# The residual's turned blocks through device memory, issued from ScalarE's queue in place of SP's

## The chip, the cores and the metric

The kernel runs on one core of a Trainium2 chip. The metric is the device time of one execution in microseconds (us). The core has five engines that run their own instruction streams and meet at semaphores: TensorE (PE in the profile, its weight loads PEld), VectorE (DVE), ScalarE (ACT), GpSimd (POOL) and SyncE (SP), which here only issues DMA transfers. A name with a q behind it (SPq, ACTq) is an engine's issuing side.

## The reference

One sequence of 256 tokens of width 1024 in float32 passes through two blocks of two layers each. All of it adds to a residual `h`.

```python
# block 1: layer 0 with gated linear attention, layer 1 with differential attention
h = h + mix(rms_norm(h, norm_mix[i]))
h = h + swiglu(rms_norm(h, norm_ffn[i]), ffn_w_in[i], ffn_w_out[i])
gate = jax.nn.sigmoid(rms_norm(h, ple_norm[i]) @ ple_w_gate[i])
h = h + gate * (p[i] @ ple_w_proj[i])
# block 2: a short convolution, then a causal attention with ALiBi and a gate
h = h + short_conv_mixer(rms_norm_2(h, norm_g[0]), conv_w_in, conv_w, conv_w_out)
h = h + moba_mixer(rms_norm_2(h, norm_g[1]), attn_w_in, q_norm_g, k_norm_g, attn_w_out)
```

Each product of a normed `h` needs `h` with the model dimension on the partitions: `h` turned. The norm's row factor is applied to the product's result, its column gain to the turned `h`.

## The kernel before

**Weights.** All weights come as one stream of 297 units of 128 x 1024 float32 (512 KB), in the order in which they are used (`TILES` and `END`, lines 48 to 69: `END[t]` is the first unit of tile t). A unit passes through a ring of four in `raw`. SP fetches it (`fetch`, line 434) once VectorE is done with the unit four before it (semaphore `w_lo`). ScalarE rounds it to `whi`, VectorE takes the rest `wlo = raw - whi`, both in rings of eight (`split_to`, lines 665 and 1075). `split_to(n)` converts all units up to n that are not yet converted, so its argument sets how far an engine runs ahead of TensorE.

**Products.** TensorE multiplies every unit in three passes, `whi` by the upper part of the turned input, `wlo` by the upper part, `whi` by the lower part (`product`, line 1753): 12 matmuls of 128 x 512. The turned inputs are the pairs `X` and `Y`, each an upper part `[0]` and a lower part `[1]` with eight slices of 128 rows (kt 0 to 7), one for each 128 columns of `h`. A unit covers two slices. It waits for the upper part of its two slices before its first matmul (`upper`, line 1780) and for the lower part before its ninth (line 1799).

**How `h` is turned.** Some slices are turned on TensorE (`h_T`, line 1870) and copied out of PSUM by `lhs_hi` and `lhs_lo`. The others take a trip through device memory. VectorE transposes 32 x 32 squares of `h` into `h_blk` (`sblk` and `gblk` are two names for it), in two halves of 256 KB. Each half is written to DRAM and read back into `h_land` in another order, which completes the transpose. ScalarE then makes the upper part with the gain in it, VectorE the lower part. There are six such trips of two halves:

- three `second_blocks` trips into a mixer or attention input: into the first feed-forward (after the first mixer), into the second one, and into the last attention's input. The half q holds slices 4 + 2q and 5 + 2q. The halves are written by `second_blk` (line 1112) and read by `second_hi` (line 697) and `second_lo` (line 1123);
- one more `second_blocks` trip into the convolution's input (`CV_IN`);
- two `gate_blocks` trips, in the middle of the gated projection of either layer. The half t holds the tokens of 128 t and the slices 0 to 3. VectorE writes it at line 1404, ScalarE reads it at line 876 and VectorE at line 1414.

First products are ordered by `PAIR_ORDER`, so that the slices of a `second_blocks` trip are wanted from the fifth unit on, half 0 for the fifth and half 1 for the sixth.

**Who issues.** SP issues all transfers of these trips, between its fetches and in program order. It stops at each of them until the block is turned (`g_blk`) and, for the way back, until the half has landed in DRAM (`g_out0`, `g_out1`). Semaphores `g_land0` and `g_land1` tell ScalarE that a half is back. `g_hi` and `g_lhs` count upper and lower parts for TensorE.

```python
for q in range(2):
    sp.wait_ge(sem("g_blk"), 2 * r + q + 1)
    sp.dma_start(s_dram[s, q], sblk[:, q, :]).then_inc(sem(f"g_out{q}"), 16)
for q in range(2):
    sp.wait_ge(sem(f"g_out{q}"), 16 * (r + 1))
    sp.dma_start(sland[:, q, :, :], s_dram[s, q]...).then_inc(sem(f"g_land{q}"), 16)
```

**The squares.** Around each trip ScalarE also squares the half of `h` that was just completed, with a sum by row for the norm (`squares` and `square`, lines 708 to 720). They write `junk` and `stats`. GpSimd makes the row factor `rstd` of them.

GpSimd issues trips of its own in the last attention: 192 KB blocks of scores, `mb_blocks` out and `mb_pT` back (lines 624 to 636).

Of the kernel before, what the change touches and what calls it, by code (L numbers as in the profile page):

```python
# [23 lines left out]
P = 128  # L24
# [51 lines left out]
LAST = ((0, 0, NW), (1, 0, NW // 2), (1, NW // 2, NW))  # L76
PAIR_ORDER = ((0, 0), (0, 1), (1, 0), (1, 1), (0, 2), (0, 3), (1, 2), (1, 3))

# [162 lines left out]
def build(nc, stream, x, p, cols_d, rows_d, consts_d, wgate_d, out):  # L241
    ctx = ExitStack()
    with ctx:
# [147 lines left out]
        gblk = hblk[:, :].rearrange("p (t n) -> p t n", t=TT)  # L391
        gland = hland[:, :, :].rearrange("p i n -> p (i n)").rearrange("p (t i n) -> p t i n", t=TT, i=P // B)

# [6 lines left out]
        s_dram = nc.dram_tensor("second_blocks", (len(PAIRED), 2, P, NW), F32, kind="Internal").ap()  # L400
        g_dram = nc.dram_tensor("gate_blocks", (2, TT, P, NW), F32, kind="Internal").ap()
# [10 lines left out]
        def _(sp):  # L412
# [79 lines left out]
            def second_blocks(r, tile):  # L492

                at = END[tile] + (7 if tile == CV_IN else 8)
                fetch(done, at)
                s = PAIRED.index(tile)
                for q in range(2):
                    sp.wait_ge(sem("g_blk"), 2 * r + q + 1)
                    sp.dma_start(s_dram[s, q], sblk[:, q, :]).then_inc(sem(f"g_out{q}"), 16)
                for q in range(2):  # L500
                    sp.wait_ge(sem(f"g_out{q}"), 16 * (r + 1))
                    sp.dma_start(sland[:, q, :, :], s_dram[s, q].rearrange("q n -> (q n)")
                                 .rearrange("(i p w) -> p i w", i=P // B, p=P)).then_inc(sem(f"g_land{q}"), 16)
                return at

            def gate_blocks(n, tile):

                at = END[tile + 2] + 8
                fetch(done, at)
                for t in range(TT):  # L510
                    sp.wait_ge(sem("g_blk"), 2 * (2 * n + 1) + t + 1)
                    sp.dma_start(g_dram[n, t], gblk[:, t, :]).then_inc(sem(f"g_out{t}"), 16)
                for t in range(TT):
                    sp.wait_ge(sem(f"g_out{t}"), 16 * (2 * n + 2))
                    sp.dma_start(gland[:, t, :, :], g_dram[n, t].rearrange("q n -> (q n)")
                                 .rearrange("(i p w) -> p i w", i=P // B, p=P)).then_inc(sem(f"g_land{t}"), 16)
                return max(done, at)

# [7 lines left out]
            for n, (out_tile, tin) in enumerate(((GLA_OUT, FFN_IN0), (DF_OUT, FFN_IN1))):  # L526
                upto(done, END[out_tile])
                done = END[out_tile]
                done = second_blocks(2 * n, tin)
# [4 lines left out]
                done = gate_blocks(n, tin + FT + 2)  # L534
            done = second_blocks(4, CV_IN)
# [15 lines left out]
            done = second_blocks(5, MB_IN)  # L551
# [108 lines left out]
        def _(act):  # L660
# [26 lines left out]

            def mixer_lhs(j, dst, out):

                split_to(END[out + 4] - 1 + AHEAD + 1)  # L690
                lhs_hi(dst, norm_gain(j), (4, 5))
                squares(j, 0)
                split_to(END[out + 4] + 1 + AHEAD)
                squares(j, 1)
                second_hi(j, dst, 2 * (j - 1) // 3, END[out + 4])

            def second_hi(j, dst, r, base):

                split_to(base + 8)
                for q in range(2):  # L700
                    act.wait_ge(sem(f"g_land{q}"), 16 * (r + 1))
                    for k in range(2):
                        kt = 4 + 2 * q + k
                        A(dst[0][:, kt, :].rearrange("p (t i b) -> p t i b", t=TT, b=B),
# [108 lines left out]
            def ffn(n, src):  # L813
# [70 lines left out]
                if n == 1:  # L884
                    second_hi(j + 1, X, 4, END[CV_IN] - 1)
# [1497 lines left out]
```

## Time and profile before

| what | us |
|---|---|
| median of 3 runs | 901.86 |
| the runs | 900.85, 903.6, 901.86 |
| the profiled execution, whole | 900.89 |
| its span, first to last instruction | 898.7 |
| TensorE busy | 892.9 |
| VectorE busy | 654.6 |
| ScalarE busy | 506.1 |
| GpSimd busy | 63.4 |

The whole time of the profiled execution is 2.2 us longer than its span. Busy time counts an engine's instructions, not its waits and not the issuing of DMA transfers. TensorE's matmuls overlap in the record, so the mean of one (about 390 ns) is longer than the distance between two. In the views below a row that says x4 has merged four instructions in a row on the engine, and the first time is the first one's start. In square brackets stands the time that the engine was idle just before, and what ended it.

### The profile page before, as it was taken

To read this page: it belongs to the slowest core of one execution; us is meant where nothing else is said; L and a number is where in the kernel's file an instruction comes from. 1 tells how busy PE (TensorE), PEld (TensorE's weight loads), DVE (VectorE), ACT (ScalarE), POOL (GpSimd) and SP (SyncE) were. 2 spreads that over 40 slices of the span, in tenths; PEclk is the share of its full clock that TensorE was granted. 3 is DMA by queue.
4 is the path that set the end of the run, shared out by engine and by line. 5 is a ranking of instruction groups with operands and counts; after the bars stand their busy time and mean duration, and the time that the engine had idled before them with its cause. 6 is when DMAs were issued, how large, how long until landed. Compare 5 with 4: busy or idle time off the path is not lost.

```text
span 898.7 us, 12238 instructions
## 1 busy us (share of the span) xinstructions
PE 892.9 (99%) x4364; PEld 737.0 (82%) x4364; DVE 654.6 (73%) x997; ACT 506.1 (56%) x820; POOL 63.4 (7%) x75
## 2 busy tenths in 40 slices
PE   9999999999999999999999999999999999999998
PEld 8988888888888888778888888888888888887777
DVE  6985478777735699997787776646679897779764
ACT  6756555444444667688564444435664544587681
POOL 0001000000000003211100000000010000215100
PEclk9999999999999999999999999999999999999999
DMA  7674458766755655424487667746568775656621
GB/s 271 197 240 143 162 189 301 277 242 243 240 194 194 227 199 201 160 97 141 139 284 265 237 239 246 254 142 231 202 220 278 260 253 192 207 200 234 227 70 47
DMA packets 76988, 187.47 MB, mean 209 GB/s; under 512 B 6852, under 2 KB 31812, under 8 KB 76936
## 3 DMA queue, kind: packets, MB, share of 16 engines
q1 hardware_dynamic: 75480, 182.99, 59.6%
q0 software_dynamic: 1024, 3.15, 1.0%
q10 hardware_dynamic: 432, 0.66, 0.2%
q8 instruction: 31, 0.51, 0.2%
q14 instruction: 21, 0.17, 0.1%
HBM read 171.83 MB, written 14.94 MB: 208 GB/s over the span
## 4 chain that ended last, share of the span: by engine, by line
PE 95%; DMA 2%; issue 2%; DVE 1%; POOL 1%; ACT 0%; DVEq 0%; POOLq 0%
PE bank L1801 84%; PE bank L1839 3%; PE bank L1854 1%; PE bank L2114 1%; PE bank L2140 1%; DMA mb_pT<-mb_blocks 1%; DMA mb_blocks<-p_tok 1%; DMA h<-x_dram 0%; PE bank L2224 0%; PE bank L2125 0%; PE bank L2253 0%; PE bank L1961 0%; PE bank L2009 0%; PE bank L2013 0%; PE bank L2100 0%
## 5 line engine op out<-in xcount | busy, mean ns | idle before, releaser
L671 ACT ACTIVATE whi<-raw 128x1024 fp32r<-128x1024 f32 x295 | 306.2, 1060 | 186.3 <-DMA raw<-stream_dram 108.8
L1079 DVE TENSOR_TENSOR wlo<-raw,whi 128x1024 fp32r<-128x1024 f32 x295 | 347.5, 1213 | 55.6 <-ACT whi L671 54.8
L1801 PE MATMUL bank<-whi,x_hi 128*128 128x512 f32 x560 | 152.5, 394 | 0.0
L1801 PE MATMUL bank<-wlo,x_hi 128*128 128x512 f32 x560 | 149.9, 389 | 0.0
L1801 PE MATMUL bank<-whi,x_lo 128*128 128x512 f32 x560 | 149.8, 389 | 0.0
L1801 PEld LDWEIGHTS bank<-wlo,x_hi 128*128 128x128 f32 x560 | 105.1, 188 | 22.3
L1801 PEld LDWEIGHTS bank<-whi,x_lo 128*128 128x128 f32 x560 | 105.1, 188 | 22.0
L1801 PEld LDWEIGHTS bank<-whi,x_hi 128*128 128x128 f32 x560 | 103.4, 188 | 21.7 <-issue 1.2
L1801 PE MATMUL bank<-whi,y_hi 128*128 128x512 f32 x396 | 108.0, 394 | 0.1
L1801 PE MATMUL bank<-wlo,y_hi 128*128 128x512 f32 x396 | 106.0, 390 | 0.0
L1801 PE MATMUL bank<-whi,y_lo 128*128 128x512 f32 x396 | 106.0, 389 | 0.0
L1801 PEld LDWEIGHTS bank<-wlo,y_hi 128*128 128x128 f32 x396 | 74.3, 188 | 15.7
L1801 PEld LDWEIGHTS bank<-whi,y_lo 128*128 128x128 f32 x396 | 74.3, 188 | 15.7
L1801 PEld LDWEIGHTS bank<-whi,y_hi 128*128 128x128 f32 x396 | 72.8, 188 | 16.0 <-issue 0.8
L824 ACT ACTIVATE ffn_silu<-bank,rstd 128x256 f32<-128x256 f32 x44 | 18.4, 471 | 76.8 <-PE bank L1801 76.8
L1303 DVE SCALAR_TENSOR_TENSOR ffn_mid<-bank,rstd,ffn_silu 128x256 f32<-128x256 f32 x44 | 19.3, 479 | 54.0 <-ACT ffn_silu L824 54.0
L1801 PE MATMUL bank<-whi,mid_hi 128*128 128x512 f32 x176 | 47.0, 389 | 0.0
L1801 PE MATMUL bank<-wlo,mid_hi 128*128 128x512 f32 x176 | 47.0, 389 | 0.0
L1801 PE MATMUL bank<-whi,mid_lo 128*128 128x512 f32 x176 | 47.0, 389 | 0.0
L1109 DVE TENSOR_TENSOR h<-h,bank 128x512 f32<-128x512 f32 x22 | 14.1, 683 | 44.7 <-PE bank L1801 44.5
L579 POOL TENSOR_TENSOR ms<-stats 128x2 f32<-128x2 f32 x8 | 4.9, 611 | 577.1 <-ACT junk L718 577.1
L1801 PEld LDWEIGHTS bank<-wlo,mid_hi 128*128 128x128 f32 x176 | 33.0, 188 | 6.9
(251 smaller groups left out, 891.4 us busy)
## 6 DMA issues: line engine op xcount, KB each, us to landing
raw<-stream_dram SPq DMA_DIRECT2D x295, 512.0 KB, 4.6
ffn_blocks<-ffn_blk SPq DMA_DIRECT2D x22, 256.0 KB, 2.0
ffn_land<-ffn_blocks SPq DMA_DIRECT2D x22, 256.0 KB, 3.7
second_blocks<-h_blk SPq DMA_DIRECT2D x8, 256.0 KB, 2.0
h_land<-second_blocks SPq DMA_DIRECT2D x8, 256.0 KB, 3.1
cv_blocks<-cv_blk SPq DMA_DIRECT2D x7, 256.0 KB, 5.2
cv_land<-cv_blocks SPq DMA_DIRECT2D x7, 256.0 KB, 3.3
h_blocks<-h_blk SPq DMA_DIRECT2D x3, 512.0 KB, 6.3
```

What stands on the lines that cost most here:

```text
L579: step(nc.gpsimd.tensor_tensor(ms[:, j, 0, :], stats[:, j, 0, :], stats[:, j, 1, :], ALU.add))
L671: A(whi[:, u % RING, :], raw[:, u % RAW, :], ACT.Copy).then_inc(sem("w_hi"), 1)
L824: A(sg[:, (t - tin) % 2, k, :], bank[2 * (t % 2) + k][:, 0:256], ACT.Silu, scale=rstd[:, j, k:k + 1]).then_inc(sem("ffn_silu"), 1)
L1079: V.tensor_tensor(wlo[:, u % RING, :], raw[:, u % RAW, :], whi[:, u % RING, :].bitcast(F32), ALU.subtract).then_inc(sem("w_lo"), 1)
L1109: V.tensor_tensor(h[:, t, half * HALF:(half + 1) * HALF], h[:, t, half * HALF:(half + 1) * HALF], bank[2 * (tile % 2) + t][:, :], ALU.add) ...
L1303: V.scalar_tensor_tensor(mid[:, (t - tin) % 2, :, k, :], bank[2 * (t % 2) + k][:, 256:512].rearrange("p (k n) -> p k n", k=2), rstd[:, j, ...
L1801: last = T.matmul(bank[pair + t][:, :], lhs[a][:, kt, t * P:(t + 1) * P], w[:, u % RING, kk * NW:(kk + 1) * NW], start=part != 1 and k == ...
L1839: last = T.matmul(bank[pair + hd // 2][:, hd % 2 * SEQ:(hd % 2 + 1) * SEQ], w[:, u % RING, kk * NW + hd * P:kk * NW + (hd + 1) * P], lhs[a ...
L1854: last = T.transpose(bank[b][:, k * SEQ + t * P:k * SEQ + (t + 1) * P], src[:, t, kt * P:(kt + 1) * P], ident)
L2114: last = T.matmul(bank[DF_S_BANKS[hd][m]][:, q * SEQ:(q + 1) * SEQ], dT[r, 0, hd, q * P:(q + 1) * P], dT[r, 1, hd, :], start=True, stop=True)
L2140: last = T.matmul(bank[b][:, q * SEQ + (hd % 2) * P:q * SEQ + (hd % 2 + 1) * P], daT[:, hd % 4, k * SEQ + q * P:k * SEQ + (q + 1) * P], dv ...
```

## The change

All 24 transfers of the six trips move from SP's queue to ScalarE's. `second_blocks` and `gate_blocks` are gone from SP's program, and its fetches run through without stopping at a trip. Each half has a name in `PIECES`, which gives its place in one DRAM tensor and its counts in the semaphores. On ScalarE `piece_out` waits for the turned block and issues the way out, `piece_in` waits for its landing in DRAM and issues the way back. At a `second_blocks` trip the order is square, out, square, out, back, conversions of weights up to the mark, back, copies. At a `gate_blocks` trip it is out, out, square, back, square, back, conversions up to the mark, copies. VectorE's and TensorE's programs keep their order; only the numbers that they wait for are written by the new names.

```diff
+PIECES = ("mix0 q0", "mix0 q1", "gate0 t0", "gate0 t1", "mix1 q0", "mix1 q1", "gate1 t0", "gate1 t1",
+          "cv q0", "cv q1", "mb q0", "mb q1")
...
-            def second_blocks(r, tile):
-
-                at = END[tile] + (7 if tile == CV_IN else 8)
-                fetch(done, at)
-                s = PAIRED.index(tile)
-                for q in range(2):
-                    sp.wait_ge(sem("g_blk"), 2 * r + q + 1)
-                    sp.dma_start(s_dram[s, q], sblk[:, q, :]).then_inc(sem(f"g_out{q}"), 16)
-                for q in range(2):
-                    sp.wait_ge(sem(f"g_out{q}"), 16 * (r + 1))
-                    sp.dma_start(sland[:, q, :, :], s_dram[s, q].rearrange("q n -> (q n)")
-                                 .rearrange("(i p w) -> p i w", i=P // B, p=P)).then_inc(sem(f"g_land{q}"), 16)
-                return at
...
+            def piece_out(name):
+
+                n = piece(name)
+                act.wait_ge(sem("g_blk"), n + 1)
+                nc.scalar.dma_start(s_dram[n], sblk[:, slot(name), :]).then_inc(sem(f"g_out{slot(name)}"), 16)
+
+            def piece_in(name):
+
+                n, q = piece(name), slot(name)
+                act.wait_ge(sem(f"g_out{q}"), 16 * turn(name))
+                nc.scalar.dma_start(sland[:, q, :, :], s_dram[n].rearrange("q n -> (q n)")
+                                    .rearrange("(i p w) -> p i w", i=P // B, p=P)).then_inc(sem(f"g_land{q}"), 16)
...
                 split_to(END[out + 4] + 1 + AHEAD)
-                squares(j, 1)
-                second_hi(j, dst, 2 * (j - 1) // 3, END[out + 4])
-
-            def second_hi(j, dst, r, base):
-
+                second_hi(j, dst, f"mix{(j - 1) // 3}", END[out + 4])
+
+            def second_hi(j, dst, name, base):
+
+                act.wait_ge(sem("h_new"), 4 * (j - 1) + 4)
+                square(j, 1, 0)
+                piece_out(f"{name} q0")
+                square(j, 1, 1)
+                piece_out(f"{name} q1")
+                piece_in(f"{name} q0")
                 split_to(base + 8)
+                piece_in(f"{name} q1")
                 for q in range(2):
...
+                    pair_hi(j, dst, f"{name} q{q}", 4 + 2 * q)
...
                     if half == 0:
 
+                        split_to(END[t + 2] + 1 + AHEAD)
+                        for k in range(TT):
+                            piece_out(f"gate{n} t{k}")
+                        square(j + 1, 0, 0)
+                        piece_in(f"gate{n} t0")
+                        square(j + 1, 0, 1)
+                        piece_in(f"gate{n} t1")
                         split_to(END[t + 2] + 2 + AHEAD)
-                        squares(j + 1, 0)
                         for k in range(TT):
-                            act.wait_ge(sem(f"g_land{k}"), 16 * (2 * n + 2))
+                            act.wait_ge(sem(f"g_land{k}"), 16 * turn(f"gate{n} t{k}"))
```

`piece(name)` is the place in `PIECES`, `slot(name)` its last digit (the half), and `turn(name)` how many pieces of the same half have come up to it.

The following pieces of the programs show what moved. First SP at the first mixer's trip, before:

```order
L438 DMA raw<-stream_dram 128x1024 [waits w_lo] x16
L499 DMA second_blocks<-h_blk 128x512 [waits g_blk] x2
L502 DMA h_land<-second_blocks 128x4x128 [waits g_out0]
L502 DMA h_land<-second_blocks 128x4x128 [waits g_out1]
L438 DMA raw<-stream_dram 128x1024 [waits w_lo] x8
```

In the changed program the four transfers are gone there and 24 fetches stand in one row. Next ScalarE in the changed program, at the convolution's input (`junk,stats<-h` is a square, `x_hi<-h_land` a copy of a half that came back):

```order
L655 ACTIVATE whi<-raw 128x1024 [waits w_used,raw3]
L725 ACTIVATE junk,stats<-h 128x512 [waits stats,h_new]
L676 DMA residual_blocks<-h_blk 128x512 [waits g_blk]
L725 ACTIVATE junk,stats<-h 128x512 [waits stats]
L676 DMA residual_blocks<-h_blk 128x512 [waits g_blk]
L682 DMA h_land<-residual_blocks 128x4x128 [waits g_out0]
L682 DMA h_land<-residual_blocks 128x4x128 [waits g_out1]
L690 ACTIVATE x_hi<-h_land,cols 128x256 [waits g_land0]
```

Before, the two squares stood one behind the other after the conversion, and the copies followed at once. At the mixers and at the last attention's input one conversion of a weight unit stands between the two transfers back. Last, ScalarE in the changed program at the first gate's trip:

```order
L655 ACTIVATE whi<-raw 128x1024 [waits w_used,raw2]
L676 DMA residual_blocks<-h_blk 128x512 [waits g_blk] x2
L725 ACTIVATE junk,stats<-h 128x512 [waits stats]
L682 DMA h_land<-residual_blocks 128x4x128 [waits g_out0]
L725 ACTIVATE junk,stats<-h 128x512 [waits stats]
L682 DMA h_land<-residual_blocks 128x4x128 [waits g_out1]
L655 ACTIVATE whi<-raw 128x1024 [waits w_used,raw3]
L888 ACTIVATE y_hi<-h_land,cols 128x128 [waits g_land0]
```

The last conversion of this row of three (`raw3`) stood ahead of the squares before.

## Rows read from the trace of the kernel before

**Rows 1.** The page: span and busy time of engines.

```profile
span 898.7 us, 12238 instructions
PE 892.9 (99%) x4364; PEld 737.0 (82%) x4364; DVE 654.6 (73%) x997; ACT 506.1 (56%) x820; POOL 63.4 (7%) x75
```

**Rows 2.** TensorE's waits: line, released by; us in total, times, longest.

```profile
PE bank L1897 <- DVE gla_r L1149: 1.2, 1, 1.2
PE bank L2253 <- DMA mb_pT<-mb_blocks: 1.1, 2, 0.7
```

**Rows 3.** Stretches, L1801's matmuls alone: length, PE and PEld busy, clock, DMA share, GB/s.

```profile
652.00:660.16 8.16, 8.16 (x37) 6.76 (x36) 1.00 0.46 168
130.86:133.58 2.72, 2.72 (x13) 2.25 (x12) 1.00 0.99 407
```

**Rows 4.** The timeline at the first mixer's trip: start, length, engine, line, what.

```profile
122.57 1.37 SPq L499 DMA_DIRECT2D second_blocks<-h_blk  x2
124.59 1.42 SPq L502 DMA_DIRECT2D h_land<-second_blocks  x2
126.05 2.38 SPq L438 DMA_DIRECT2D raw<-stream_dram  x4
...
127.41 0.91 ACT L704 ACTIVATE x_hi<-h_land,cols 128x256 fp32r<-128x256 f32 x2 [3.48 <-DMA h_land<-second_blocks]
...
130.86 1.07 PE L1801 MATMUL bank<-whi,x_hi 128*128 128x512 f32 x4
```

**Rows 5.** The timeline at the first gate's trip.

```profile
317.31 2.04 SPq L512 DMA_DIRECT2D gate_blocks<-h_blk  x2
319.39 2.09 SPq L515 DMA_DIRECT2D h_land<-gate_blocks  x2
...
325.08 1.28 ACT L876 ACTIVATE y_hi<-h_land,cols 128x128 fp32r<-128x128 f32 x4 [1.48 <-DMA h_land<-gate_blocks]
...
327.61 0.70 PE L1801 MATMUL bank<-whi,y_hi 128*128 128x512 f32 x2
```

**Rows 6.** ScalarE's timeline at the convolution's input.

```profile
656.00 1.06 ACT L671 ACTIVATE whi<-raw 128x1024 fp32r<-128x1024 f32 x1 [0.20 <-DMA raw<-stream_dram]
656.97 0.62 ACT L718 ACTIVATE junk<-h 128x512 f32<-128x512 f32 x1
...
660.57 0.91 ACT L704 ACTIVATE x_hi<-h_land,cols 128x256 fp32r<-128x256 f32 x2 [2.13 <-DMA h_land<-second_blocks]
```

**Rows 7.** TensorE's timeline at the convolution's input, fifth unit.

```profile
662.88 1.07 PE L1801 MATMUL bank<-whi,x_hi 128*128 128x512 f32 x4
```

**Rows 8.** Transfers by line: ns min/median/max to issue, first and last start; then their landing.

```profile
L499 SPq DMA_DIRECT2D second_blocks<-h_blk x8: 326/326/327, 122.6 to 765.8; - x8
...
DMA to landing us min/median/max: 2.0/2.0/2.0
...
L502 SPq DMA_DIRECT2D h_land<-second_blocks x8: 370/371/371, 124.6 to 767.8; - x8
...
DMA to landing us min/median/max: 2.6/3.1/4.3
...
L634 POOL DMA_DIRECT2D mb_pT<-mb_blocks x8: 747/759/772, 810.1 to 847.0; - x8
...
DMA to landing us min/median/max: 3.2/5.3/5.9
...
L741 ACTq DMA_DIRECT2D raw<-stream_dram x1: 444/444/444, 0.7 to 0.7; - x1
```

**Rows 9.** SP's timeline at the convolution's input.

```profile
655.88 1.37 SPq L499 DMA_DIRECT2D second_blocks<-h_blk  x2
657.90 1.42 SPq L502 DMA_DIRECT2D h_land<-second_blocks  x2
```

More of the change, by code:

```diff
@@ L76, with piece, slot, turn @@
 LAST = ((0, 0, NW), (1, 0, NW // 2), (1, NW // 2, NW))
+PIECES = ("mix0 q0", "mix0 q1", "gate0 t0", "gate0 t1", "mix1 q0", "mix1 q1", "gate1 t0", "gate1 t1",
+          "cv q0", "cv q1", "mb q0", "mb q1")
 PAIR_ORDER = ((0, 0), (0, 1), (1, 0), (1, 1), (0, 2), (0, 3), (1, 2), (1, 3))
+def piece(name):
+    return PIECES.index(name)
+def slot(name):
+    return int(name[-1])
+def turn(name):
+    return sum(slot(other) == slot(name) for other in PIECES[:piece(name) + 1])
 def done_at(tile):
@@ L533, in _ @@
                 done = half_blocks(n, tin + FT)
-                done = gate_blocks(n, tin + FT + 2)
-            done = second_blocks(4, CV_IN)
+                fetch(done, END[tin + FT + 4] + 8)
+                done = END[tin + FT + 4] + 8
             fetch(done, done_at(CV_IN) + 10)
@@ L550, in _ @@
             done = max(done, END[MB_IN])
-            done = second_blocks(5, MB_IN)
             fetch(done, UNITS)
@@ L1123, in second_lo, with pair_blk @@
-            def second_lo(j, dst, r, base):
+            def pair_blk(name, news, kt0, first):
+                for t in range(TT):
+                    if first:
+                        dve.wait_ge(sem("h_new"), news + t + 1)
+                    at = slice(kt0 * P, (kt0 + 2) * P)
+                    last = V.transpose(sblk[:, slot(name), :].rearrange("p (f k t b) -> p t f k b", f=P // B, k=2, t=TT)[:, t],
+                                       h[:, t, at].rearrange("p (k b f) -> p f k b", b=B, f=P // B))
+                last.then_inc(sem("g_blk"), 1)
@@ new lines, in pair_lo @@
+            def pair_lo(j, dst, name, kt0):
+                n = piece(name)
+                for k in range(2):
+                    kt = kt0 + k
+                    dve.wait_ge(sem("g_hi"), 2 * n + k + 1)
+                    for t in range(TT):
+                        at = slice(t * P, (t + 1) * P)
+                        part = sland[:, slot(name), :, :].rearrange("p i (k t b) -> p k t i b", k=2, t=TT)[:, k, t]
+                        last = V.scalar_tensor_tensor(dst[1][:, kt, at].rearrange("p (i b) -> p i b", b=B), part,
+                                                      norm_gain(j)(kt),
+                                                      dst[0][:, kt, at].bitcast(F32).rearrange("p (i b) -> p i b", b=B),
+                                                      ALU.mult, ALU.subtract)
+                last.then_inc(sem("g_lhs"), 1)
@@ L1859, in lhs_T, with piece_need, second_need @@
                 return need
-            def second_need(r):
-                return [("g_lhs", 2 * r + q + 1, ("g_hi", 4 * r + 2 * q + 2)) for q in range(2)]
+            def piece_need(name):
+                return ("g_lhs", piece(name) + 1, ("g_hi", 2 * piece(name) + 2))
+            def second_need(name):
+                return [piece_need(f"{name} q{q}") for q in range(2)]
             def first_tiles(tile, lhs, signal, need, beside=None):
@@ L2082, in ffn @@
                 product(tple + 2, src, "ple_sig")
-                half1 += [("g_lhs", 2 * (2 * n + 1) + k + 1, ("g_hi", 4 * (2 * n + 1) + k + 3)) for k in range(2)]
+                r = piece(f"gate{n} t0")
+                half1 += [("g_lhs", r + k + 1, ("g_hi", 2 * r + k + 3)) for k in range(2)]
                 product(tple + 3, PT, "ple_gated")
```

89 lines of the change are left out of this document (30 added, 59 removed).

## The prediction

> **What bounds the kernel now.** I read the busy times first. TensorE is busy for 892.9 of the span's 898.7 us, ScalarE for 506.1 us, 56% [rows 1]. The kernel is paced by its matmuls, and any other engine can change the time only where it makes TensorE wait or ends a wait of TensorE's. So the second view is TensorE's own waits: the longest is 1.2 us at the start, the next are two waits of 1.1 us in all, for the score blocks that GpSimd sends through device memory in the last attention [rows 2]. None is for a residual block or a weight. The third view is TensorE's busy time by stretch: between 652.00 and 660.16 us, when two trips of the residual were on their way, it was busy for 8.16 of 8.16 us, at the full granted clock [rows 3]. A weight unit of 12 matmuls takes 2.72 us there as elsewhere [rows 3], which is three units in 8.16 us and no gap. So nothing is lost at the trips today, and moving them can win nothing there. What it can do is make a block late. The question is therefore how much slack each trip has: from the copy that frees TensorE to the matmul that reads it.
>
> **What one trip looks like.** At the first mixer SP issues the two transfers out from 122.57 us and the two back from 124.59 us, and only then fetches weights again, at 126.05 us, four in a burst [rows 4]. ScalarE makes the first upper parts from 127.41 us, having waited 3.48 us for the landing. This pair of copies ends at 127.41 + 0.91 = 128.32, and TensorE reads it at 130.86 us: 2.5 us of slack [rows 4]. The second mixer and the last attention's input repeat this pattern. The first gate trip has less: its second half starts to be copied at 325.08 us, half of its four copies are enough for the next unit (0.7 us), and TensorE reads at 327.61 us, so 1.8 us [rows 5]. The tightest is the convolution's input: copies from 660.57 for 0.91 us end at 661.48, and TensorE reads at 662.88 us: 1.4 us [rows 6, 7].
>
> **Step 1, issues leave SP.** 24 transfers leave SP, at 0.33 us out and 0.37 us back [rows 8]. SP no longer stands waiting for the turned blocks, so the weight fetches behind them can go as soon as a slot is free. That is worth nothing by itself, since TensorE waits for no weight. It has a side effect: at the first mixer the fetches went at 126.05 us, behind both transfers back [rows 4]. Now they go beside them.
>
> **Step 2, issues enter ScalarE.** An issue on ScalarE took 0.44 us in the one kind that the trace shows [rows 8]. 24 of them are 10.6 us of ScalarE, which has 898.7 - 506.1 = 392.6 us free [rows 1]. In each trip they stand where ScalarE waited 2 to 3.5 us for the landing anyway [rows 4, 6]. What counts is the order: a transfer out now follows a square. Two squares with their readouts ran from 656.97 us to the start of the wait at 660.57 - 2.13 = 658.44 us, so one takes 0.74 us [rows 6].
>
> At the mixers ScalarE arrives early. The first square is over before the first block is turned, so the first transfers out and back leave as now: no delay. The second one back stands behind one weight unit's conversion (1.06 us in the row at 656.00 [rows 6]) and leaves about 0.5 us later. Slack 2.5 us: no cost.
>
> At the gates ScalarE waits for both blocks before its first square. The second block was ready at 317.31 + 2.04 - 0.33 = 319.02 us, and the second transfer back left at 319.39 + 2.09 - 0.37 = 321.1 us [rows 5]. Now an issue, a square, an issue and a square follow on the second block before that transfer can leave, 0.44 + 0.74 + 0.44 + 0.74, so 321.4 us: 0.3 us later against 1.8 us of slack. No cost. One conversion of a weight unit moves behind the squares there. Its unit is read several units on, so the ring of eight converted units hides it.
>
> At the convolution's input it is different. SP issued the first transfer out at 655.88 us, and ScalarE began its squares only at 656.97 us, held by a conversion from 656.00 us that had waited for its weights [rows 6, 9]. In the changed order the transfer out cannot go before the first square is done. If ScalarE arrives as today that is 656.97 + 0.74 = 657.7 us, 1.8 us late. With fetches freed a little it may arrive up to a microsecond sooner. I take half of that: out at 657.25 us, landed 2.0 us later [rows 8], back issued at 659.25 us where it was 657.90 us [rows 9].
>
> **Step 3, how long a transfer back takes beside weight fetches.** Lower bound: as now, 2.6 to 4.3 us with a median of 3.1 [rows 8]. Upper bound: the nearest rows of a trip on a queue of its own beside the weights, GpSimd's, which take 3.2 to 5.9 us for a block of three quarters the size [rows 8]. I take 3.7 us, half way between the 3.1 us median and the 4.3 us of the slowest of today's, which had a weight burst right behind it: one fetch or two will be beside it, not a full queue. The chain at the convolution's input is then 659.25 + 3.7 + 0.91 = 663.86 against TensorE's 662.88 us [rows 7]: a stall of 1.0 us. With 2.65 us and ScalarE early it is zero. With 5.9 us and ScalarE as late as today or a little later (back at 660.3 us) it is 660.3 + 5.9 + 0.91 - 662.88 = 4.2 us. At the gates 5.9 us gives 321.4 + 5.9 + 0.7 - 327.61 = 0.4 us each. At the mixers it gives 124.6 + 5.9 + 0.91 - 130.86 = 0.55 us, at three places less than 0.6 us each.
>
> The Trainium skill, page "DMA: Bandwidth & Descriptors", section "Issuing engines are not separate DMA queues", says that transfers issued by different engines run on the same 16 DMA engines and interleave, so that a second issuing engine saves only the time of issuing. By that rule the whole benefit would be SP's issue time, which is not on the path here, and the sum would be the same or worse. The rows on TensorE's waits agree as to the benefit [rows 2].
>
> **The sum.** SP's part 0, ScalarE's issues 0, mixers and last input 0, gates 0, convolution's input +1.0 us. The profiled execution took 900.89 us, with its span of 898.7 us, so it would be 901.9 us. The median of the runs shown is 901.86 us, so I predict 902.9 us. About 0.3%, 2.7 us, is what a measurement of this kernel can tell from no change: its own three runs lie 2.75 us apart.
>
> **Rivals.**
> *Wholly hidden.* ScalarE reaches the squares a microsecond earlier because weights were fetched sooner, and the transfers back take what they take now. For it: TensorE has no wait there today, and ScalarE waits 2.13 us for the landing [rows 6], so part of its order is free. Time 901.9 us.
> *Slower, through the shared DMA engines.* The transfers back no longer have the DMA engines to themselves, since the weight fetches that stood behind them on SP now go beside them. It decides from the point where a transfer back takes over 2.7 us plus what is left of the slack, at the convolution's input about 2.7 us, at the first mixer 5.3 us. For it: GpSimd's trips at 5.3 us median, and the two waits of TensorE's that they cause [rows 2, 8]. Against it: at the moment of issue only one fetch or two can be under way, since VectorE turns the blocks just before and frees no slot meanwhile. At 5.9 us everywhere the places add up to 4.2 + 0.8 + 1.6 = 6.6 us, in a mixed case to 3 to 4 us: 905.5 us. The extreme: a block comes back in 512 pieces of 128 numbers; if each waits for a row of 4 KB of weights, 2.1 MB pass at the 407 GB/s of a stretch full of weights [rows 3], 5.2 us, and with the 2.0 us of the shortest transfer 7.2 us; by the same subtractions some 12 us in all, 914 us.
> The Trainium skill, same page, section "Queues, rings and completion order", says that an engine takes turns between the queues packet by packet, which is this rival's extreme. The trace has no transfer from ScalarE's queue beside weights, so no run here shows it.
> *Faster.* The only waits that a shift of the weight stream could remove are GpSimd's, 1.1 us [rows 2]: 900.8 us, which is no difference that can be told. Over 2.7 us faster has no source in the waits.
> *Not what it says.* If SP's old waits return through the weights' own semaphores (it waits for slots anyway), the transfers stay alone and only the order on ScalarE counts: again between 0 and 1.8 - 1.4 = 0.4 us.
>
> **How the numbers follow.** My forecast, a stall of some 1 us and at most 2.7 us, gets 0.45; wholly hidden, with the last rival, 0.27. Both are within 0.3%: 0.72. Slower through the DMA engines 0.22, of it 0.05 for the extreme. Over 0.3% faster 0.06, for what the spread of the runs alone can do. The range begins at 900.8 us (hidden, and runs as the lowest of those shown, 900.85) and ends at 905.6 us (the mixed case of the rival); the extreme stays outside.
>
> **What would show it.** TensorE's waits should have at most one new row, on the matmul line, released by ScalarE's copy of the residual near 663 us, around 1 us long. ScalarE's transfers out should land in 2.0 us, those back in 3 to 4.5 us, and SP should no longer wait for h_blk except for the half blocks. TensorE at 652 to 661 us should still be busy throughout. I am wrong if the transfers back take over 5 us, if TensorE waits at the mixers too, or if its waits fall below those of before by more than 1.1 us.

## The result and the profile after

The changed kernel takes 908.64 us (median of 8 runs, 905.26 to 909.72) against 901.29 us (8 runs, 900.38 to 903.6) of the kernel before on the same chip. The ratio is 1.0073, 95% interval 1.0057 to 1.0089. It goes by all runs, whose means are 908.0 and 901.5 us; the medians are 7.3 us apart. The kernel is slower by 0.7 to 0.8%. The prediction had 902.9 us and a range of 900.8 to 905.6 us, so the result lies outside. The profiled execution took 909.12 us with a span of 907.1 us, 8.4 us more than the span of before [rows 1].

The page of the profile: span and busy time of the engines.

```profile
span 907.1 us, 12236 instructions
PE 895.3 (99%) x4364; PEld 738.6 (81%) x4364; DVE 654.8 (72%) x997; ACT 505.1 (56%) x820; POOL 66.7 (7%) x75
```

ScalarE and VectorE do what they did before. TensorE's waits say where the time went (line, released by; us in total, times, longest):

```profile
PE bank L1823 <- ACT ple_gate L873: 3.9, 2, 2.5
PE bank L1823 <- ACT y_hi L690: 2.3, 1, 2.3
PE bank L1922 <- DVE gla_r L1171: 1.2, 1, 1.2
PE bank L2279 <- DMA mb_pT<-mb_blocks: 1.2, 1, 1.2
```

The last two answer to [rows 2] and are nearly unchanged in total (1.2 us each, where it was 1.2 and 1.1). The first two are new, 6.2 us: both gates and the second mixer. The convolution's input, the one place that the prediction named, is not among them. ScalarE's transfers by line (ns min/median/max to issue, first and last start, then their landing) answer to [rows 8]:

```profile
L676 ACTq DMA_DIRECT2D residual_blocks<-h_blk x12: 332/338/350, 122.9 to 774.1; - x12
...
DMA to landing us min/median/max: 2.0/2.1/3.2
...
L682 ACTq DMA_DIRECT2D h_land<-residual_blocks x12: 372/392/404, 125.0 to 776.2; - x12
...
DMA to landing us min/median/max: 2.7/5.5/6.7
```

The way out is as fast as it was, the way back went from a median of 3.1 us to 5.5 us. The timeline at the first gate, where [rows 5] show SP's order before:

```profile
319.74 0.39 ACTq L682 DMA_DIRECT2D h_land<-residual_blocks  x1
...
320.57 4.16 SPq L464 DMA_DIRECT2D raw<-stream_dram  x4
...
321.43 0.37 ACTq L682 DMA_DIRECT2D h_land<-residual_blocks  x1
...
328.06 1.28 ACT L888 ACTIVATE y_hi<-h_land,cols 128x128 fp32r<-128x128 f32 x4 [3.92 <-DMA h_land<-residual_blocks]
...
329.24 1.24 ACT L873 ACTIVATE ple_gate<-bank,rstd 128x512 f32<-128x512 f32 x2
...
330.58 1.95 PE L1823 MATMUL bank<-whi,y_hi 128*128 128x512 f32 x4 [2.50 <-ACT ple_gate L873]
```

The weight fetches start at 320.57 us, before the second transfer back, which lands after 6.6 us. Behind ScalarE's four copies stand two sigmoids that empty the banks of the tile before (`ple_gate`, the array `sig` of the code). TensorE goes on 0.1 us after these. Here is the piece of the kernel before's timeline that the prediction should have had:

```profile
325.08 1.28 ACT L876 ACTIVATE y_hi<-h_land,cols 128x128 fp32r<-128x128 f32 x4 [1.48 <-DMA h_land<-gate_blocks]
...
326.26 1.24 ACT L867 ACTIVATE ple_gate<-bank,rstd 128x512 f32<-128x512 f32 x2
```

The sigmoids ended at 326.26 + 1.24 = 327.50 us and TensorE began the next tile at 327.61 us [rows 5]. The gate trip had no slack before the change, though TensorE showed no wait there.

There is a third loss. Stretches with length, busy time, granted clock, DMA share and GB/s, in the changed kernel:

```profile
328.00:330.50 2.50, 0.07 (x1) 0.00 (x0) 1.20 (x4) 2.44 (x7) 0.00 (x0) 1.00 0.26 103
330.50:331.00 0.50, 0.42 (x1) 0.41 (x2) 0.49 (x1) 0.50 (x1) 0.00 (x0) 0.68 0.12 41
331.00:334.00 3.00, 3.00 (x8) 2.32 (x7) 3.00 (x5) 3.00 (x4) 0.00 (x0) 0.50 0.01 3
334.00:336.00 2.00, 2.00 (x14) 1.74 (x13) 2.00 (x3) 0.64 (x2) 0.00 (x0) 0.98 0.34 82
```

After TensorE had stood still for 2.5 us it resumed at a granted clock of 0.50, its level of 1.2 GHz, and did 8 matmuls in 3 us. The lost cycles are 0.5 x 0.32 + 3 x 0.50 + 2 x 0.02 = 1.7 us. Waits of 6.2 us and a slow stretch of 1.7 us are 7.9 of the 8.4 us. All eight runs of the changed kernel have a mean clock below 1.0, four of 0.998 and four of 0.996, which is one or two such stretches in 907 us. In the 60 runs of the kernel before that were made beside the experiments below it is 1.0. Only the stretch of the profiled execution can be placed.

Two more places of the changed kernel. The second mixer:

```profile
450.79 0.34 ACTq L676 DMA_DIRECT2D residual_blocks<-h_blk  x1
...
453.98 0.40 ACTq L682 DMA_DIRECT2D h_land<-residual_blocks  x1
...
460.59 1.71 ACT L690 ACTIVATE y_hi<-h_land,cols 128x256 fp32r<-128x256 f32 x4 [5.06 <-DMA h_land<-residual_blocks]
...
461.55 1.20 PE L1823 MATMUL bank<-whi,y_hi 128*128 128x512 f32 x4 [2.31 <-ACT y_hi L690]
```

Here the transfer out took 3.2 us as well (450.79 to 453.98), with weights of earlier fetches still on their way until about 451.5 us; that these delayed it is likely and not shown. The transfer back took 6.6 us (453.98 to 460.6). The convolution's input:

```profile
663.54 0.34 ACTq L676 DMA_DIRECT2D residual_blocks<-h_blk  x1
663.59 0.63 ACT L725 ACTIVATE junk<-h 128x512 f32<-128x512 f32 x1
...
665.62 1.39 ACTq L682 DMA_DIRECT2D h_land<-residual_blocks  x2
...
670.11 0.91 ACT L690 ACTIVATE x_hi<-h_land,cols 128x256 fp32r<-128x256 f32 x2 [5.04 <-DMA h_land<-residual_blocks]
...
671.07 1.19 PE L1823 MATMUL bank<-whi,x_hi 128*128 128x512 f32 x4
```

The copies end at 670.11 + 0.91 = 671.02 us and TensorE reads at 671.07 us. The slack is used up there too, and it just held. The first two lines show one thing more: the transfer out stands behind the square in ScalarE's program, and yet its issue starts at 663.54 us, before the square has even begun. It waits for the turned block and not for the square.

### The profile page after: what moved, and what is told of

Read it like the earlier page. It is cut to its first block, busy times and chain, and to the rows that moved or that the text cites. A ratio compares the mean times of both kernels' runs of the same rounds, so it can differ in the third digit from the quotient of the medians.

```text
span 907.1 us, 12236 instructions
## 1 busy us (share of the span) xinstructions
PE 895.3 (99%) x4364; PEld 738.6 (81%) x4364; DVE 654.8 (72%) x997; ACT 505.1 (56%) x820; POOL 66.7 (7%) x75
## 4 chain that ended last, share of the span: by engine, by line
PE 92%; DMA 4%; DVE 2%; issue 1%; POOL 1%; ACT 1%; DVEq 0%; ACTq 0%; POOLq 0%
PE bank L1823 80%; PE bank L1861 3%; DMA h_land<-residual_blocks 2%; PE bank L1876 1%; PE bank L2140 1%; DMA residual_blocks<-h_blk 1%; PE bank L2166 1%; PE bank L2250 1%; DMA mb_pT<-mb_blocks 1%; PE bank L2279 1%; DVE h_blk L1426 0%; PE bank L2151 0%; PE bank L1922 0%; PE bank L1986 0%; PE bank L2034 0%
## 5 line engine op out<-in xcount | busy, mean ns | idle before, releaser
L1823 PEld LDWEIGHTS bank<-whi,mid_lo 128*128 128x128 f32 x176 | 33.0, 188 | 6.9
```

Source lines behind the costliest of these rows:

```text
L1823: last = T.matmul(bank[pair + t][:, :], lhs[a][:, kt, t * P:(t + 1) * P], w[:, u % RING, kk * NW:(kk + 1) * NW], start=part != 1 and k == ...
```

## The experiments

Theory A: the transfers back, now on a queue of their own, share the DMA engines with the weight fetches and take turns with them. Its rivals: ScalarE's order delays the trips; ScalarE's issues cost time; a transfer from its queue is slow as such. The table has the medians, and the ratio over all runs to the kernel before on the same chip (its medians are 901.29 us beside the changed kernel and 901.35, 901.29 and 901.16 us in the groups x1 to x4, x5 to x8, x9 and x10). The last column is the execution that the profile shows, which in x1, x4, x6 and x9 lies well off the median:

| kernel | median us (runs) | ratio, 95% interval | profiled us |
|---|---|---|---|
| changed kernel | 908.64 (8) | 1.0073, 1.0057 to 1.0089 | 909.12 |
| x1 fetches held | 904.13 (10) | 1.0027, 1.0017 to 1.0038 | 901.05 |
| x2 order only | 901.45 (10) | 1.0008, 0.9996 to 1.0020 | 900.75 |
| x3 back only | 914.19 (4) | 1.0150, 1.0123 to 1.0177 | 912.62 |
| x4 gates on SP | 903.63 (10) | 1.0043, 1.0021 to 1.0065 | 906.89 |
| x5 = x3, plain rows | 902.07 (10) | 1.0002, 0.9993 to 1.0012 | 902.7 |
| x6 = changed, plain rows | 905.49 (6) | 1.0044, 1.0030 to 1.0058 | 907.5 |
| x7 out only | 901.23 (10) | 0.9995, 0.9985 to 1.0004 | 901.74 |
| x8 only gates on ScalarE | 907.14 (4) | 1.0073, 1.0046 to 1.0100 | 907.59 |
| x9 = changed, sigmoids early | 905.18 (5) | 1.0057, 1.0030 to 1.0083 | 908.88 |
| x10 = before, sigmoids early | 901.59 (10) | 0.9998, 0.9987 to 1.0010 | 901.91 |

**x1, the fetches held.** SP waits at each of the six trips until both halves are back, ahead of its next fetches:

```diff
+            def hold(name, at):
+                fetch(done, at)
+                for q in range(2):
+                    sp.wait_ge(sem(f"g_land{q}"), 16 * turn(f"{name}{q}"))
+                return at
...
+                done = hold(f"mix{n} q", END[tin] + 8)
```

> The changed kernel, with SP holding its weight fetches at each of the six trips until both halves are back. Theory A (the transfers back, on a queue of their own, share the DMA engines with weight fetches that no longer stand behind them; they took 2.7 to 6.7 us where they took 2.6 to 4.3): transfers back fall to about 2.7 to 3.7 us, TensorE's waits for y_hi and for the gate's unit go, time 901 to 903 us. Rival B (it is ScalarE's order: issues behind squares, waits for landings ahead of conversions): nothing of that is changed, time stays 907 to 909 us.

All transfers stay on ScalarE's queue in ScalarE's order. Their landing, and TensorE's waits:

```profile
L691 ACTq DMA_DIRECT2D h_land<-residual_blocks x12: 377/377/389, 124.6 to 768.4; - x12
...
DMA to landing us min/median/max: 2.6/2.8/3.4
```

```profile
PE bank L1832 <- ACT y_hi L675: 0.8, 1, 0.8
PE bank L2288 <- DMA mb_pT<-mb_blocks: 0.6, 1, 0.6
```

With no new fetch beside them the transfers back take 2.6 to 3.4 us, and the slowdown falls from 0.73% to 0.27%. So neither ScalarE's queue nor its issues are slow, and most of the cost comes from the fetches beside the transfers. The median is 1.1 us above the 901 to 903 us that theory A expected. What the rest is stays open: the fetches now start later, which may be it, but the profiled execution is the fastest of the ten, no slower than the kernel before, and shows no wait for it. Three of the ten have a mean clock of 0.998.

**x2, the order only.** All 24 transfers stay on SP, with waits that give ScalarE's order of the change: the transfer out behind the square, the second one back behind the weight conversion or the second square.

```diff
                     sp.wait_ge(sem("g_blk"), 2 * r + q + 1)
+                    sp.wait_ge(sem("stats"), 4 * j + 3 + q)
                     sp.dma_start(s_dram[s, q], sblk[:, q, :]).then_inc(sem(f"g_out{q}"), 16)
...
                     sp.wait_ge(sem(f"g_out{q}"), 16 * (r + 1))
+                    if q:
+                        sp.wait_ge(sem("w_hi"), base + 8)
...
```

> The kernel before with all transfers on SP, but each only once ScalarE has passed the same square or conversion as in the changed kernel, and ScalarE with the changed kernel's waits and order. So the order of the change without its queue. Theory A: 901 to 902.5 us. Rival B: 906 to 909 us.

901.45 us, transfers back of 2.7 to 4.5 us. The order alone costs nothing that can be told. Here SP waits until the squares are done, which is stricter than the changed kernel, where ScalarE's issue goes beside the square.

**x3, only the way back.** From the kernel before: SP still issues the transfers out and waits for them, ScalarE issues the twelve back.

```diff
                 for q in range(2):
                     sp.wait_ge(sem(f"g_out{q}"), 16 * (r + 1))
-                    sp.dma_start(sland[:, q, :, :], ...)
...
+                for q in range(2):
+                    act.wait_ge(sem(f"g_out{q}"), 16 * (r + 1))
+                    nc.scalar.dma_start(sland[:, q, :, :], ...)
                 split_to(base + 8)
```

> The kernel before with only the 12 transfers back issued by ScalarE, at once when the halves have landed in DRAM; SP still issues the ways out and holds its fetches until they have landed. The weights start within about 0.7 us of where they started before, but on another queue than the transfers back. Theory A in its narrow form (the separate queue is what costs, since the transfers back no longer go first): the transfers back take 4 to 6.5 us, time 904 to 908 us. Rival C (it is the early fetches that cost, not the queue): transfers back 2.6 to 4.3 us, 901 to 902 us.

914.19 us, worse than the change itself and than the 904 to 908 us that theory A expected. The first mixer:

```profile
124.69 1.45 ACTq L698 DMA_DIRECT2D h_land<-second_blocks  x2
...
125.77 3.14 SPq L438 DMA_DIRECT2D raw<-stream_dram  x4
...
134.66 0.51 ACT L705 ACTIVATE x_hi<-h_land,cols 128x256 fp32r<-128x256 f32 x1 [6.42 <-DMA h_land<-second_blocks]
```

SP had stood waiting while slots of `raw` came free, so it sends a burst of four fetches at the moment at which the second half starts back (125.74 us). In the kernel before it did so too, at 126.05 us [rows 4], 0.3 us later, but there the burst stood behind both transfers back in one queue and they took 4.3 us at most [rows 8]. So it is not that the fetches come early (rival C); it is that they no longer wait their turn behind the transfer. At the first mixer the second half takes 8.9 us, at the second 9.5, at the convolution's input 8.9 us. The DMA view of 127.5 to 133.5 us, while the second half was on its way at the first mixer (queue, packets, MB, share of the 16 engines; q1 is SP's queue, q10 ScalarE's):

```profile
q1 hardware_dynamic: 525, 1.95, 83.2%
q10 hardware_dynamic: 511, 0.26, 14.3%
```

511 pieces of 512 bytes on one queue and 525 packets, nearly all pieces of 4 KB, on the other: one for one. The half moves 0.26 MB in the time in which the weights move 1.95 MB. In each 0.2 us from 128.0 to 129.0 us, right from where the half begins to move, there are 14 to 18 pieces of the half and 14 to 19 packets of the weights; turns of many pieces each would come in bunches. This is the turn-taking that the Trainium skill states in "DMA: Bandwidth & Descriptors", section "Queues, rings and completion order". The trace agrees that the engines take turns. What the page calls a packet typically holds 9 to 17 descriptors; the trace's even counts of 0.2 us fit single pieces in turn, and the measurement decides here.

**x5, x3 with plain rows.** The transfer back reads its half as it lies, 128 rows of 2 KB, in place of 512 pieces of 512 bytes. The reordering that completes the transpose is left out, here and in x6, so these two kernels compute other values; only their times are of use.

```diff
-    s_dram[s, q].rearrange("q n -> (q n)").rearrange("(i p w) -> p i w", i=P // B, p=P)
+    s_dram[s, q].rearrange("q (i w) -> q i w", i=P // B)
```

> x3_back_only with one thing changed: the twelve transfers back read their half as it lies, 128 rows of 2 KB, in place of 512 pieces of 512 bytes. The bytes, the queue and the place in ScalarE's program are the same. The reordering of the blocks within each half is left out, so the second half of each left-hand side holds its values in another order. Theory A, turn by turn: a piece of a transfer back waits for a piece of a weight fetch (a row of 4 KB) at each turn of a DMA engine; 512 turns made 8.9 us beside a burst of four fetches, 128 turns cost a quarter of the added time: 128 x 4 KB = 0.5 MB at 407 GB/s = 1.3 us, so each transfer back takes 3 to 4.5 us and the kernel 901 to 904 us. Rival B, the transfer lands only when the weight bytes that are queued with it are through, whatever its pieces are: the second backs stay at 8 to 9.5 us and the time at 912 to 916. Rival C, bandwidth is shared by bytes: 256 KB beside weights take twice their own time at any piece size, so 5 us at most already in x3, which its 8.9 us speak against.

902.07 us: the whole loss of x3 is gone, with the same bytes on the same queue at the same place. The landings of the four `second_blocks` trips:

```profile
L698 ACTq DMA_DIRECT2D h_land<-second_blocks x8: 326/337/351, 125.4 to 769.3; - x8
...
DMA to landing us min/median/max: 2.5/3.8/5.0
```

The second half at the first mixer lands after 5.0 us where x3 took 8.92 us. That is 3.9 us less for 384 fewer pieces, or 24 fewer on each of 16 engines: 0.163 us a piece. A piece of 4 KB at a sixteenth of 407 GB/s [rows 3] is 0.161 us. So one turn costs about one weight piece. Theory A had expected 3 to 4.5 us; there is some 1 us more beside a burst than its turns explain. A queue that lets a transfer land only when the queued weights are through (rival B) is refuted.

**x6, the changed kernel with plain rows.** The same edit on the changed kernel.

> The changed kernel with the same edit: the twelve transfers back read 128 rows of 2 KB, and the reordering within each half is left out. Theory A: transfers back of 2.5 to 4 us in place of 4.5 to 6.7, no TensorE wait at the first gate or the second mixer, 901 to 904 us. Rival B: transfers back as in the changed kernel and 906 to 909 us.

Neither theory had this: 905.49 us, and transfers back of 2.7 to 6.0 us with a median of 4.5 us, where the changed kernel has 5.5 us. TensorE still waits 2.9 us at the gates and 1.9 us at the second mixer in the profiled execution, the slowest of the six.

```profile
L682 ACTq DMA_DIRECT2D h_land<-residual_blocks x12: 326/327/392, 125.5 to 774.0; - x12
...
DMA to landing us min/median/max: 2.7/4.5/6.0
```

Here the number of pieces is only part of the price. At the first gate most of the late half is through by 325 us in both kernels. The DMA view of the changed kernel from 322.4 to 325 us, and behind it from 325 to 328.1 us:

```profile
q1 hardware_dynamic: 163, 0.61, 65.5%
q10 hardware_dynamic: 420, 0.21, 26.8%
...
q1 hardware_dynamic: 323, 1.20, 95.1%
q10 hardware_dynamic: 108, 0.05, 7.0%
```

Some hundred of the half's 512 pieces still trickle in among 323 packets of the weights, and the half has landed only when its last piece has. In x6 from 325 to 327.6 us it is 32 packets of 128. Which engines these are and why they lag stays open.

**x7, only the way out.** The counterpart of x3: ScalarE issues the transfers out between its squares, SP those back.

> The counterpart of x3_back_only: only the twelve transfers out (128 rows of 2 KB) are issued by ScalarE, in the changed kernel's places between its squares; the transfers back stay on SP, behind its waits on the transfers out, so that no new fetch is beside either. Theory A: the fetches queued before a transfer out are still on their way, so it takes 2.0 to 3.2 us, the transfers back 2.6 to 4.5 as before, 901 to 903 us. If the trips through ScalarE's queue were slow as such, or ScalarE's twelve issues (0.33 us each) cost time, 904 to 906.

901.23 us, transfers out of 2.0 to 2.1 us, back of 2.7 to 4.1 us. Twelve issues and the squares in between cost ScalarE nothing that shows.

**x4 and x8, the gates apart.** x4 is the changed kernel with the gates' four pairs of transfers on SP again, x8 the changed kernel with everything but these on SP again.

```diff
                 fetch(done, END[tin + FT + 4] + 8)
+                for t in range(TT):
+                    m = piece(f"gate{n} t{t}")
+                    sp.wait_ge(sem("g_blk"), m + 1)
+                    sp.dma_start(s_dram[m], sblk[:, t, :]).then_inc(sem(f"g_out{t}"), 16)
...
-                            piece_out(f"gate{n} t{k}")
```

> The changed kernel with its two gate trips back on SP in the old order, the other four trips on ScalarE. In the changed kernel's trace the waits near 327.7 us (2.7 us) and near 658 us (1.6 us) belong to the gates and the one near 459 us (2.5 us) to the second mixer. If the places add up, this wins 3 to 4.3 us of some 7: 904 to 905.5 us. If the convolution's input was covered only by the stall before it, a new wait of 1 to 2 us comes up near 663 us and the time is 905 to 907 us.

> The complement of x4_gates_on_sp: the changed kernel with the trips of the two mixers, the conv input and the last attention input back on SP, so that only the two gates' four trips are on ScalarE's queue. The wait at the first gate (2.7 us in the changed kernel) and at the second (1.6 us) should stay, and the one of 2.5 us at the second mixer go. Theory A: 903.5 to 906.5 us. If the stages don't add up, and the delay is only passed from one to the next, within 1 us of the kernel before or of the changed one.

The parts don't add up: 0.43% without the gates, 0.73% with the gates alone, 0.73% with both. The intervals are wide, though, and x4's runs fall into two groups, six of 902.1 to 904.0 us and four of 906.9 to 909.6 us. Its median of 903.63 us lies below both ranges that were expected. In x4's profiled execution, the fastest of the upper group, the second mixer no longer waits and the convolution's input does, twice:

```profile
662.87 0.38 ACTq L691 DMA_DIRECT2D h_land<-residual_blocks  x1
...
663.62 0.91 ACT L699 ACTIVATE x_hi<-h_land,cols 128x256 fp32r<-128x256 f32 x2 [4.37 <-DMA h_land<-residual_blocks]
...
664.58 1.21 PE L1826 MATMUL bank<-whi,x_hi 128*128 128x512 f32 x4 [1.08 <-ACT x_hi L699]
...
669.21 1.20 PE L1826 MATMUL bank<-whi,x_hi 128*128 128x512 f32 x4 [1.57 <-ACT x_hi L699]
```

For the convolution's input this fits a TensorE that is held at the gate just before and gives the trip slack; x9 below agrees. It does not explain the second mixer, which waits in the changed kernel and in x9 and not in x4; why is open. x8 was expected at 903.5 to 906.5 us for theory A and came out 0.6 us above. Its profiled execution has 3.1 us of waits at the gates, and its longest wait is one of 2.4 us for the score blocks (1.1 us in [rows 2]), with a stretch of half clock behind it. That wait also comes to 1.9 us in the traces of x7 and x10, which are no slower than the kernel before, so a part of x8's loss may not be the gates'.

**x9 and x10, the sigmoids ahead.** At each gate the two sigmoids of the second half stand ahead of the wait for the trip's second half. x9 has this in the changed kernel, x10 in the kernel before.

```diff
-                for half in range(2):
+                for half in range(1):
...
                         for k in range(TT):
+                            if k:
+                                split_to(END[tple + 3] + AHEAD - 2)
+                                c.wait(act, "w_used", END[tple + 3])
+                                act.wait_ge(sem("ple_gated"), TT * (2 * n + 1))
+                                for kk in range(TT):
+                                    A(sig[:, kk, :], bank[2 * ((tple + 2) % 2) + kk][:, :], ACT.Sigmoid, scale=rstd[:, j, kk:kk + 1])\
+                                        .then_inc(sem("ple_sig"), 1)
                             act.wait_ge(sem(f"g_land{k}"), 16 * turn(f"gate{n} t{k}"))
```

> The changed kernel with one move in ScalarE's program at either gate: the pair of sigmoids that frees two PSUM banks (1.24 us, line 873) stands ahead of the wait for the trip's second half, not behind the copies that follow this wait. Theory G: at the gates the late half costs what it does because these sigmoids are queued behind it, and TensorE waits for the banks; in the kernel before they ended at 326.26 + 1.24 = 327.50 us and TensorE went on at 327.61 us, so that the gate trips had no slack at all, where the prediction counted 1.8 us. Then TensorE needs only the first two of the four copies: it goes on at 328.06 + 0.64 + 0.1 = 328.8 us in place of 330.58 us at the first gate, and with no wait or one under 0.3 us at the second. The stretch of half clock behind the first gate should go as well. 3.4 us from the waits and up to 1.7 us from the clock: 903.5 to 906 us. Rival: the landing itself is the limit, through the lower parts that VectorE makes from it, and the time stays at 907 to 909.5 us.

> The kernel before with the same move. Theory G: nothing waits there today, so 901.3 us and within 0.1% of the kernel before; a gain of over 1 us or a loss would mean that the move does something else than to give slack.

x9 at the first gate:

```profile
324.98 1.27 ACT L889 ACTIVATE ple_gate<-bank,rstd 128x512 f32<-128x512 f32 x2 [1.26 <-PE bank L1828]
...
326.77 1.28 ACT L893 ACTIVATE y_hi<-h_land,cols 128x128 fp32r<-128x128 f32 x4 [0.53 <-DMA h_land<-residual_blocks]
...
327.71 1.17 PE L1828 MATMUL bank<-whi,y_hi 128*128 128x512 f32 x4
```

Its transfers back take as long as in the changed kernel (2.9 to 7.1 us), though at this gate 5.8 us (321.01 to 326.77) in place of 6.6. TensorE doesn't wait here; at the second gate 0.4 us is left. In the old order the sigmoids would have come behind these copies and ended at 326.77 + 1.18 + 1.24 = 329.2 us, 1.5 us after TensorE's start at 327.71 us (an estimate, with the 1.18 us from the first copy to the sigmoids of the changed kernel). So most of the gates' 3.9 us came from what stood behind the landing. Much of it comes back later:

```profile
PE bank L1828 <- ACT y_hi L690: 2.8, 1, 2.8
...
PE bank L1828 <- ACT x_hi L690: 0.8, 1, 0.8
```

At the second mixer TensorE waits 2.8 us where it was 2.3 us, and at the convolution's input 0.8 us where it was nothing. All of TensorE's waits together fall only from 8.9 to 8.2 us, and this execution took 908.88 us against 909.12 us. The median of five runs, 905.18 us, is 3.5 us lower and within what was expected, but the intervals of the two ratios overlap: that the move wins time is not shown, only that it takes away the gates' wait. x10 changes nothing, as expected. None of the ten beats the kernel before by what can be told.

## Why the prediction was wrong

*What bounds the kernel* was right: TensorE's busy time sets the span, and the change could win nothing.

Two steps failed, the slack at the gates and the time of a transfer back in step 3. In the sum they are the terms "gates 0", where 3.9 us came, and "mixers and last input 0", where 2.3 us came. The prediction's own signs of being wrong both came: the transfers back took over 5 us (median 5.5), and TensorE waited at a mixer.

*The slack of the trips* was wrong at the gates. The prediction had 1.8 us there, from the landing to TensorE's reading of `y_hi`, and counted only the copies. TensorE also waits for two banks that ScalarE empties behind these copies, and that ended 0.1 us before TensorE's start. The slack was 0.1 us at most. x9 shows it by taking just this away. At the mixers "2.5 us, the pattern repeats" was about right for the first and the last, which show no wait. It was not enough at the second, where the transfer out took 3.2 us too.

*Step 1* named the side effect, fetches beside the transfers back, and left its price to step 3. It is the mechanism of most of the loss: x1 takes it away and leaves 0.27% of 0.73%, and x3, with the burst right beside the second half, makes it worse.

*Step 2, the issues on ScalarE.* 0.44 us was too high; they take 0.34 us out and 0.39 us back, 12 x 0.73 = 8.8 us in all, and hidden. The order was right in that it costs nothing by itself (x2, x7). "The transfer out cannot go before the first square is done" was wrong: it went at 663.54 us, when its block was turned, and the square ran from 663.59 to 664.22 us beside it. So the forecast of a first transfer out 1.4 us late at the convolution's input had no ground: in the changed kernel it left 663.54 - 660.00 = 3.5 us after the tile's first matmul, where it had been 655.88 - 652.00 = 3.9 us. The stall of 1.0 us that the sum had there did not come.

*Step 3, the time of a transfer back*, was mis-sized: 3.7 us against a median of 5.5 us. The reason given, "one fetch or two will be beside it, not a full queue", does not hold for the late halves. At the first gate 0.61 + 1.20 = 1.8 MB of weights passed from 322.4 to 328.1 us, which is 3.5 fetches of 0.52 MB, and beside the second halves at the first mixer and at the convolution's input it was 1.47 and 1.37 MB, nearly three. New fetches kept coming while the transfer was under way, and it had no place ahead of them. The upper bound of 5.9 us from GpSimd's rows was passed by three of the twelve (up to 6.7 us).

At a gate the long transfer makes the loss, and the missing slack doubles it. With 3.7 us the second half would have landed at 321.43 + 3.7 = 325.1 us, where it was copied before the change (325.08 us), and nothing would have been lost. With the long transfer and the slack of the prediction the landing at 328.06 us would have cost 328.06 + 0.7 - 327.61 = 1.2 us, where TensorE waited 2.5 us.

*The rival "slower, through the shared DMA engines"* is what happened. Its case with 5.9 us everywhere gave 6.6 us, near the measured 7.3 us, and that is luck: it put 4.2 us at the convolution's input, where nothing was lost, 0.8 us at the gates, where 3.9 us were, and nothing on the clock, where 1.7 us were. The mixed case, which set the end of the range, was 3 us too low. It got 0.22 and should have had most of the chance, for the only trips that the trace showed on a queue of their own beside weights had a median of 5.3 us [rows 8]. Its extreme, one weight row for each piece, is what x3 shows, which is not the change: 8.9 us where 7.2 us was worked out.

*The clock* was in no step. A wait of over 2 us was priced at its own length, though what follows it can run at half clock: 1.7 us in the profiled execution. By the mean clocks it happened once or twice in every run.

*Wholly hidden* (0.27 with the last rival) fell with the result: the transfers back did not take what they had taken. *Not what it says* fell too: SP fetched at 320.57 us where it had been 321.83 us.

## What to carry to other kernels

A small strided transfer that someone waits for is best put on the queue of the bulk fetches, ahead of them. On a second queue each of its pieces can wait for a bulk piece. Holding the fetches for it helps only in part (x1, still 0.27% slower). Before costing a delay, follow the engine that waits for the landing to the end of what is queued behind the wait, and see who needs that; a place without a wait can have a slack of only 0.1 us. A stall of TensorE can cost more than its own length, since a stretch of half clock may follow it.

## What the runs showed of the hardware

- Two queues that both have work share an engine piece by piece: 511 pieces of 512 bytes against 525 packets of mostly 4 KB in 6 us (x3), and 0.163 us less for each turn less (x5 against x3).
- The same bytes in pieces of 2 KB in place of 512 bytes land in 5.0 us (x5) in place of 8.9 us (x3) beside a burst of weights. The fastest of either kind, with little beside it, took 2.5 and 2.6 us.
- A stall of 2.5 us of TensorE was followed by 3.4 us at a granted clock of 0.50. The one of 2.3 us at the second mixer was not (clock 1.00 throughout from 457 to 465 us).
- ScalarE issues a transfer beside its own running instruction: the transfer out of 663.54 us, behind the square in the program, was issued before the square had begun, and the one of 664.58 us within the square of 664.34 to 664.97 us. What held both was the turned block.
